# Unequal token split by a runtime branch, forget bias inside the exponential, PV by query rows, and projections between attention units

## What is computed

```python
h = rmsnorm(x, norm_g)
z = h @ w_in                     # 2048 -> 7176 columns: q k v (1024 each) f (8) gA u vB gB (1024 each)
logf = log_sigmoid(z_f + b_f)    # one forget value per token and head
s = q.k * 128**-0.5 + cum[t] - cum[s]      # cum: running sum of logf; causal, 8 heads x 128
att = softmax(s) @ v
out_a = att * silu(gA)
out_b = gelu(u) * (W_s @ layernorm(gelu(vB)) + b_s) * silu(gB)  # W_s lower triangular, 128x128, chunks of 128
y = rmsnorm(x + concat(out_a, out_b) @ w_out, final_g)
```

## Time and profile before

| | |
|---|---|
| median of 3 runs | 1996.45 us (1995.67 to 2056.99) |
| the profiled execution, span of its slowest core | 1993.9 us (cores: 1979.1 to 1993.9) |
| PE / PE weight load / DVE / ACT / POOL busy | 1786.0 / 916.8 / 790.0 / 724.4 / 209.4 us |
| bytes moved by the core's DMA queues | 187.73 MB, mean 94 GB/s |
| instructions | 31025 |

### The profile page before, as it was taken

The page is one execution under the profiler, slowest core; times in us unless marked ns, Lnnn a source line. Parts: engine busy times, 40 slices in busy tenths (PEclk is TensorE's granted clock), DMA queues, the critical chain, the costliest instruction groups (busy, mean ns, idle before and its releaser), DMA issues.

```text
span 1993.9 us, 31025 instructions; the slowest of 8 cores (1979.1 to 1993.9 us)
## 1 busy us (share of the span) xinstructions
PE 1786.0 (90%) x10577; PEld 916.8 (46%) x10721; DVE 790.0 (40%) x1349; ACT 724.4 (36%) x1303; POOL 209.4 (11%) x221
## 2 busy tenths in 40 slices
PE   2699999999999999999899958888888888879997
PEld 1255554555545555444455534444344444434443
DVE  0122222333332000144222347778777877623333
ACT  1134443222212121355222216666566655411111
POOL 4011111000021111033100000110111011100000
PEclk9799999999999999999999989999999999989999
DMA  7965664444459666100532042541453155344342
GB/s 162 151 170 159 174 167 131 96 95 104 105 79 152 101 94 101 40 1 1 55 33 21 1 80 64 97 81 28 86 97 76 26 93 75 74 139 157 139 169 90
DMA packets 220978, 187.73 MB, mean 94 GB/s; under 512 B 180688, under 2 KB 192480, under 8 KB 211408
## 3 DMA queue, kind: packets, MB, share of 16 engines
q1 hardware_dynamic: 110472, 139.56, 25.2%
q0 software_dynamic: 110352, 46.18, 20.5%
HBM read 172.12 MB, written 59.65 MB: 116 GB/s over the span
## 4 chain that ended last, share of the span: by engine, by line
PE 77%; DVE 11%; DMA 5%; issue 3%; ACT 1%; POOL 1%; DVEq 0%; SPq 0%; another core or an unknown queue 0%; ACTq 0%; POOLq 0%
PE psb L684 22%; PE psb L440 12%; PE psb L1183 11%; PE psb L430 11%; DVE arena L1093 6%; PE psb L741 6%; PE psb L1068 4%; PE psb L994 3%; PE psb L992 3%; DMA arena<-w_in 3%; PE psb L1072 1%; PE psb L415 1%; DVE arena L1044 1%; DVE arena L1039 1%; DMA arena<-w_out 1%
## 5 line engine op out<-in xcount | busy, mean ns | idle before, releaser
L684 PE MATMUL psb<-arena 128*128 128x416 bf16 (+1 forms) x2560 | 451.6, 339 | 8.7 <-ACT arena L697 5.5
L1032 ACT ACTIVATE arena<-psb 128x512 bf16<-128x512 f32 (+3 forms) x656 | 307.4, 534 | 145.7 <-DVE arena L1039 79.0
L684 PEld LDWEIGHTS psb<-arena 128*128 128x128 bf16 x2560 | 250.4, 98 | 206.3 <-issue 12.9
L440 PE MATMUL psb<-arena 128*128 128x512 bf16 (+1 forms) x1024 | 248.4, 382 | 19.0 <-DMA arena<-w_in 16.4
L1068 PE MATMUL psb<-arena 128*128 128x512 bf16 (+3 forms) x615 | 217.8, 355 | 43.0 <-ACT arena L1032 42.2
L992 PE MATMUL psb<-arena 128*128 128x512 bf16 (+3 forms) x618 | 219.7, 356 | 37.1 <-DVE arena L1039 33.5
L1183 PE MATMUL psb<-arena 128*128 128x512 bf16 (+1 forms) x1067 | 236.5, 382 | 17.8 <-DMA arena<-w_out 16.5
L994 PE MATMUL psb<-arena 128*128 128x512 bf16 (+1 forms) x639 | 227.0, 355 | 24.7 <-DMA arena<-ones_b 23.6
L430 PE MATMUL psb<-arena 128*128 128x512 bf16 (+1 forms) x1024 | 233.3, 385 | 10.2 <-DMA arena<-w_in 5.7
L1183 PEld LDWEIGHTS psb<-arena 128*128 128x128 bf16 (+1 forms) x1088 | 106.5, 98 | 148.1 <-issue 21.8
L430 PEld LDWEIGHTS psb<-arena 128*128 128x128 bf16 (+1 forms) x1056 | 102.7, 99 | 129.9 <-issue 16.0
(11 more groups left out here) (169 smaller groups left out, 1605.1 us busy)
## 6 DMA issues: line engine op xcount, KB each, us to landing
arena<-x_own SPq DMA_DIRECT2D x32, 1024.0 KB, 8.1
arena<-x_oth SPq DMA_DIRECT2D x16, 1024.0 KB, 7.9
arena<-w_in POOLq DMA_DIRECT2D x32, 512.0 KB, 7.9
y_own<-arena SPq DMA_DIRECT2D x16, 1024.0 KB, 4.8
arena<-w_in POOLq DMA_DIRECT2D x48, 256.0 KB, 27.5
arena<-KT_s SPq DMA_DIRECT2D x8, 1028.0 KB, 5.5
k_own<-arena SPq DMA_DIRECT2D x16, 512.0 KB, 4.8
v_own<-arena SPq DMA_DIRECT2D x16, 512.0 KB, 3.1
```

The costliest lines, as they stand in the source:

```text
L440: PE.op(lambda k=k, c=c: nc.tensor.matmul(PSB[4 + c][0:rows, :], hT[:, k, :], WV[:, k, c * 512:(c + 1) * 512], start=(k == 0), stop=(k == ...
L684: PE.op(lambda k=k, b=b, c0=c0, n=n: mm(PSB[b][:, 0:n], ring[s][:, k, :], H[:, k, c0:c0 + n], start=(k == 0), stop=(k == KC - 1)), reads=r ...
L1032: ACT.op(lambda: nc.scalar.activation(out=Pb[pi][0:rows, off:off + n], in_=PSB[b][0:rows, off:off + n], func=AF.Exp, scale=SCALE), reads=[ ...
```

## The change

The kernel is rewritten. Two core types ("roles") are in one program; `emit` is called for both behind a runtime branch on an input, `role`. Two cores share one stream as before: role 0 owns blocks 0 to 19 and no samples, role 1 owns blocks 20 to 31 and two sample streams (32 rows, `NS2`). Causality lets role 0 do without K and V of blocks 20 to 31; role 1 computes K and V of all 32 blocks. The host hands over x also transposed, and the weights cut and laid out by chunk.

- **Norm and K/V**: x comes transposed (`xT`), 2 blocks a load pair into three tiles; squares on ACT, sums on DVE, over partitions by f32 matmuls with ones, `rsqrt` as exp(-0.5 ln); 16 DVE multiplies make h. No transposes. K is made transposed, two heads x 256 tokens a unit; role 0 makes K of all its blocks first, then V. V is stored with a 129th column of 2.0.
- **gMLP v, u, gB, mixing**: as before, without q and gA; silu is made as (1 + tanh(x/2)) x, the factor 2 taken out elsewhere. They come before q and gA now.
- **Sweep**: no bias matmul and no mask matmul: exp has scale and a per-partition bias (`nb`, per query tile, key block and head), POOL zeroes above the diagonal. PV has P as the stationary operand, 128 query rows at a time, and V with its 129th column moving: the output has queries on partitions, its last column is twice the denominator. `fin` normalises and gates, `tr` transposes back, the result goes to HBM (`oT_s`).
- **Projections between units**: q and gA of head h+1 are cut into single matmuls (`qga`, a generator) and are emitted between the units of head h (`fill`). gA has tokens stationary and 128 weight columns moving.
- **Output**: as before, its left operand loaded from `oT_s` in groups of 4 blocks; output weights are loaded during the sweep as space comes free.

```diff
-    def e_S(i): ...  PE.op(... KTh x Qh ...); PE.op(... A_all x Bh, the bias ...); if diag: PE.op(... mneg_b ...)
-    def e_PV(i): ... PE.op(lambda: mm(PSB[ab][:, off:off + n], Vh[p][:, u["kb"], :], Pb[pi][:, off:off + n], ...
+    rv = nc.values_load(io["role"], min_val=0, max_val=1,
...
+    with nc.If(rv == 0):
+        emit(ctx, 0)
+    with nc.Else():
+        emit(ctx, 1)
...
+    if role == 0:
+        groups = [("own", list(range(4 * i, 4 * i + 4))) for i in range(NT)]
+        passes = [("K", i) for i in range(NT)] + [("V", i) for i in range(NT)]
...
+    NKS = 3                      # buffers Kf (f32) and Kb (bf16) of K units
...
+    def norm_b(n):
...
+        for c in range(2):
+            mmop(PSB[7][:, 0:w], ones[:, :], ssp[:, c, 0:w], c == 0, c == 1, [ones.r, ssp.r], 7, c == 0, c == 1)
+        ACT.op(lambda: act.activation(out=r[:, 0:w], in_=PSB[7][:, 0:w], func=AF.Ln, scale=1.0 / D, bias=RMS_EPS),
...
+        for k in range(KC):
+            DVE.op(lambda k=k: v.scalar_tensor_tensor(out=dst[:, k, :]..., in0=x[:, :, k, :], scalar=gcol[:, k:k + 1], in1=r[:, 0:w]..., 
...
+    def k_unit(gi, i0, cnt, heads):
...
+                mmop(PSB[bank][:, hi_ * w:(hi_ + 1) * w], WK[h][:, k, :], hv[:, k, :], ...
...
+            ACT.op(lambda: act.activation(out=Kf[s][:, 0:tot], in_=PSB[bank][:, 0:tot], func=AF.Copy),
...
+            POOL.op(lambda: g.tensor_copy(out=Kb[s][:, 0:tot], in_=Kf[s][:, 0:tot]), reads=[Kf[s].r], writes=[Kb[s].r])
...
+            store(SP, io["kT"]..., fv, Kf[s].r)
...
+            for i0 in (0, 2):
+                need_pair(gi, i0)
+                for h in range(0, 8, 2):
+                    if h == 4:
+                        norm_slot()          # norm_b of the next pair, x_next() (loads), norm_a of the one after
...
+                    k_unit(gi, i0, 2, [h, h + 1])
...
+    def qga(h):
...
+                mmop(PSB[b][:, 0:n], w[:, k, :], H[:, k, c0:c0 + n], ...          # q, 512 (role 1: 392) columns
+                    yield n / 2.4 + 3
...
+                    mmop(PSB[b][0:rows, i * 128:(i + 1) * 128], H[:, k, j * 128:j * 128 + rows], w[:, k, :], ...   # gA, 128 columns
+                        yield 56
...
+    LA = 2
...
+    def e_S(i):
...
+        b = i % 2
...
+            mmop(PSB[b][:, off:512], KTh[p][:, j * 128:(j + 1) * 128], Qh[p][:, T * 512 + off:(T + 1) * 512], True, True,
...
+            ACT.op(lambda: act.activation(out=P[:, off:512], in_=PSB[b][:, off:512], func=AF.Exp, scale=SCALE, bias=nb[:, T, j, h:h + 1]),
...
+            if dd >= 0:
+                POOL.op(lambda: g.affine_select(out=P[:, off:off + 128], ...
...
+    def e_PV(i):
...
+            for q in range(q0, 4):
+                b = ob + q // 2
+                mmop(PSB[b][:, (q % 2) * 256:(q % 2) * 256 + 129], P[:, q * 128:(q + 1) * 128], Vh[p][:, j, :],
...
+    def fill(finish=False):
...
+        filler["credit"] += filler["rate"]
+        while finish or filler["credit"] > 0:
...
+                filler["credit"] -= next(filler["gen"])
...
+            if i % nu_head == 0:
+                fill(finish=True)
+                if h == 7:
+                    A.free(H, *ring)
+                    f_setup()
+                else:
+                    filler.update(gen=qga(h + 1), credit=0.0, rate=fcost / (nu_head - 2))
...
+            e_S(i)
+        if i >= LA:
+            e_PV(i - LA)
+        flush(i - LA)
+        fill()
```

More of the change, by code:

```diff
@@ new lines, in v_unit @@
+        store(SP, io["V_s"].rearrange("h t j c -> t h j c")[:, :, j, :], Vb[s][:, :, :], Vb[s].r, R_Vs)
+    x_next()
+    for h in range(8):
+        load(POOL, WK[h][:, :, :], io["wk"][h], WK[h].r)
+    load(SP, bfb[:], io["bf"].partition_broadcast(128), bfb.r)
+    if smp:
+        POOL.op(lambda: g.memset(Vn[:, :, 128:129], 2.0), pwrites=[Vn.r])
+    load(POOL, wf[:, :, :], io["wf"], wf.r)
+    for c in range(len(WV)):
+        for hf in range(2):
+            load(POOL, WV[c][:, hf * 8:(hf + 1) * 8, :], io["wv"][c][:, hf * 8:(hf + 1) * 8, :], WV[c].r, part=(hf == 1))
@@ new lines, in emit, with ring_fill @@
+    assert state["pos"] == len(order)
+    A.free(*(Kb + Vb))
+    if role == 0:
+        A.free(*(Kf + Vf))
+    else:
+        A.free(*(xt[0:2] + sq + [ssp] + rb + hTb))
+    chunks = []
+    for gi in range(8):
+        chunks += [("wu", gi), ("wgb", gi)]
+    for h in range(8):
+        chunks += [("wq", h), ("wga", h)]
+    ring = [A.alloc("ring%d" % s, [KC, 128], BF16) for s in range(NRING)]
+    ring_state = {"loaded": 0, "used": 0}
+    def ring_fill():
+        while ring_state["loaded"] < min(len(chunks), ring_state["used"] + NRING):
+            i = ring_state["loaded"]
+            nm, idx = chunks[i]
+            load(POOL, ring[i % NRING][:, :, :], io[nm][idx], ring[i % NRING].r)
+            ring_state["loaded"] += 1
@@ new lines, in emit @@
+    for (rows, a, b) in parts:
+        ACT.op(lambda: act.activation(out=tzf[0:rows, a:b], in_=tzf[0:rows, a:b], func=AF.Ln, bias=1.0), reads=[R_L], writes=[R_L])
+    for (rows, a, b) in parts:
+        DVE.op(lambda: v.tensor_scalar(out=tzf[0:rows, a:b], in0=tzf[0:rows, a:b], scalar1=-1.0, scalar2=None, op0=ALU.mult),
+               reads=[R_L], writes=[R_L])
+    store(SP, io["lf"][:, o0:o0 + no, :], tz[:, o0:o0 + no, :], R_L)
+    if smp:
+        store(SP, io["lfs"], tz[0:NS2, kb, :], R_L)
+        lfc = A.alloc("lfc", [2, 16, 8], F32)
+        load(SP, lfc[:, :, :, :], io["clf"].rearrange("s p j h -> p s j h"), lfc.r)
@@ new lines, in mixing @@
+            DVE.op(lambda: v.tensor_tensor(out=t[:, 0:n], in0=t[:, 0:n], in1=Ub[p][:, c0:c0 + n], op=ALU.mult), reads=[t.r, Ub[p].r], writes=[t.r])
+            DVE.op(lambda: v.tensor_tensor(out=o[:, 0:n], in0=t[:, 0:n], in1=Gb[p][:, c0:c0 + n], op=ALU.mult), reads=[t.r, Gb[p].r], writes=[o.r])
+            store(SP, io["oT_s"][8 + gi, :, c0:c0 + n], o[:, 0:n], o.r, R_oT[8 + gi][ti])
+    for gi in range(8):
+        c_chunk("wu", gi)
+        if gi >= 1:
+            mixing(gi - 1)
+        c_chunk("wgb", gi)
@@ L1192, in build_program @@
         so = 40 + p * 4
-        ss, sd, rs = [sml[0:rows, so + i:so + i + 1] for i in range(3)]
-        ACT.op(lambda: nc.scalar.activation(out=junkF[0:rows, :], in_=yb[p][0:rows, :], func=AF.Square, accum_out=ss),
-               reads=[R_yb[p]], writes=[R_junkF, R_ssF[p]])
-        ACT.op(lambda: nc.scalar.activation(out=sd, in_=ss, func=AF.Sqrt, scale=1.0 / D, bias=RMS_EPS), reads=[R_ssF[p]], writes=[R_ssF[p]])
-        DVE.op(lambda: v.reciprocal(out=rs, in_=sd), reads=[R_ssF[p]], writes=[R_ssF[p]])
@@ L1249, in make_in_maps @@
+            ckT=c(cache_k[sm].transpose(0, 2, 3, 1)), cvn=c(cache_v[sm].reshape(2, 16, 128, 8, 128).transpose(0, 3, 2, 1, 4)),
+            clf=c(cache_lf[sm].reshape(2, 16, 128, 8).transpose(0, 2, 1, 3)))
+        for r in range(2):
+            mr = dict(m)
+            mr["role"] = np.full((1, 1), r, np.int32)
+            in_maps.append(mr)
     return in_maps
```

1958 lines of the change are left out of this document (910 added, 1048 removed).

## The result

The changed kernel takes 1659.12 us (median of 4 runs, 1657.52 to 1662.02) against 1996.82 before: ratio 0.8311, 95% interval 0.8298 to 0.8324. The forecast was 1625 us, its range 1560 to 1740. The profiled execution spans 1655.4 us.

What follows compares the result with a forecast made beforehand. TensorE bounds the kernel, 90% busy, with DVE holding the sweep. Role 0: 858 us to the sweep, 468 for it, 10 wait, 277 output, 10 tail make 1623, plus 2.5: 1625 us; range 1560 to 1740.

Steps and rivals of the forecast that it cites:

- The mechanism: Whole kernel: fewer matmul columns on TensorE and a sweep no longer held by DVE; 371 us less.
- Rival (b): Matmuls of 128 or 129 columns: slower in long streams, at most +192 us, 1817; chance 0.08.
- (a): K pass: DMA-bound at the old mean of 168 GB/s, 27.4 us a pair, +67, 1692; chance 0.14.
- (c): Sweep: projections hide nothing, units keep the old 0.90 us pace, 679 instead of 468, 1836; chance 0.07.
- (d): Sweep: TensorE waits so often that its clock is halved; heads 0 to 6 +416, 2041; chance 0.04.
- the unseen cost: Table reloads, named with a K period of 23 us for the own range's upper end, 1670 us.
- V 146 (stores 16 MB, 110 GB/s, hidden): V pass of role 0: 20 blocks at 7.29 us of TensorE, 146 us, its stores hidden.
- B to C keeps its stall of about 8 us: Before the sweep: the last LayerNorm chain still frees the space, so TensorE waits about 8 us.
- The SP loop: K pass: x loads wait for the norm, kT stores queue behind, ACT's copy waits for them; 20 us a pair.
- a DVE loop: K pass: the norm's multiplies and sums on DVE's path allow 16 to 17 us a pair at best.
- the 65 that I had set as a limit: Sweep: the forecast is wrong if a head takes over 65 us.
- Role 1 was wrong: Split of cores: role 1 needs about 1420 us of TensorE, ends near 1545; role 0 longest by some 80.

Runs made afterwards that it cites:

- The layout experiment: Changed kernel with V's scratch laid out by token, 2064 bytes a run instead of eight runs of 258: 1626.55 us.
- the late weights: Changed kernel with role 0 issuing gMLP v's weights (8.4 MB) after 12 V units instead of ahead of them: 1648.2 us.
- the late loads: Changed kernel with x loads issued after a pair's last K unit, and sums of squares as two additions: 1637.21 us, one execution.
- the combination: Changed kernel with V scratch by token, wsf moved, sums as additions, late x loads, transposes in the finished tile's bank: 1597.21 to 1600.08 us.
- the 8-row matmul of zeros: Changed kernel with a second matmul, 8 rows of zeros, into each unit's score bank, at the forget-bias matmul's place: 1889.02 us.

## Why the prediction was right, and where it was not

**The mechanism and the size were right**: the forecast was 34 us short of 1659, 2%. TensorE's sum for role 0 was 1473; PE is busy 1493.5. Part of the closeness is luck: in the table by stage the rows that ran over make 59 us together and those that ran under 27.

**Rival (b), slow narrow matmuls, is out.** The end of head 0's q and all its gA, one piece of the chain:

```profile
851.47 24.30 PE psb L291 x349
```

29 matmuls of 512 at 0.2166 are 6.3 us; the 18.0 left over 320 of 128 columns are 0.0563 each, within 2% of the short burst's 0.0556 in the earlier trace rows. The Trainium skill ("TensorE: Matmul & The Clock Gate", section Back-to-back issue gap) has about 81 ns there; the measurement decides against it for this stream.

**Rivals (a), (c), (d).** The K pass took 19.6 us a pair on the average of nine, not 27.4. In its steady part, 91 to 200 us, the DMA engines moved 170 GB/s, 3.1 MB a pair and not 4.6, at a share of 0.50: they were not the bound there, though they were nearly full in the two long pairs (0.98 and 0.87). The projections hide the units' latencies: undoing it costs 91 us. The granted clock is 1.00 in heads 0 to 6, with PE busy 94% of the time (I had said over 95), and 0.95 in head 7, with 79%: nothing like the half speed of (d).

**No table reloads in the sweep**, the unseen cost I bounded at 42 us: one load ahead of 480 exponentials and 40 tanh.

```profile
L1026 ACT ACT_TABLE_LOAD x1 | 1.3, 1283 | 0.0
```

**The step that failed: "V 146 (stores 16 MB, 110 GB/s, hidden)".** I costed the stores by bytes, and left out the 8.4 MB of gMLP v's weights that come in beside them. By runs they were 20,137 packets of under 512 bytes, at a share over 1.0 with 136 GB/s moved. The layout experiment takes the V stall away, all but 3.3 us of the second, and 37 us off core 4; the late weights moved the V stall with them, so the short runs stalled TensorE only together with the weights. The Trainium skill ("DMA: Bandwidth & Descriptors", section Specifications) names 512 bytes as the least for line rate and so speaks against this store; the traces agree (2.0 against 9.5 us for the same bytes). "B to C keeps its stall of about 8 us" found its successor one stage earlier: before gMLP v, 16.4 us, by an overlay of buffers that I had not followed. The 8 us I had kept after gMLP v for the last LayerNorm chain were not needed: u, gB and mixing ran 9 under. The row that I took them from did not name that chain either: it gives 5.5 of its 8.7 us to ACT's L697 and 3.2 to a load of w_in.

**The K pass** came near (176 us for nine pairs, 180 forecast) by luck. The SP loop that I described is there (the late loads show it), but the period was shared with a DVE loop whose sums I had 0.7 us too low each, and both were about 18. Two waits of some 20 us for a kT store, in no term of mine, made up the difference.

**The sweep**: a head took 63.3 us, under the 65 that I had set as a limit, 61.2 forecast. PE's busy time was as summed (59.5 a head, 59.4 forecast); it sat idle 3.8 us a head where I had allowed 1.8. Of that, 1.9 is its wait behind the copy of transposed tiles, which I did not name, and 0.8 its wait for the diagonal mask on POOL. A full exponential took 687 ns, not 630: I had added the 0.09 to 0.537, busy time over count, and not to the row's mean of 0.607. It cost nothing where PE sets the pace and up to 3 us (60 times 0.057) in head 7.

**Role 1 was wrong**: I had it end 80 us before role 0, and it ended 9 to 22 before. PE is busy 1488.5 us on core 1, 68 more than my sum; some 30 of these lie in 910 to 1455, where PE is busy 520 and my prices make about 490. I never laid role 1 out stage by stage, and which of its operations were costed too low is not settled. The forecast stood since role 0 still ended last; the combination ends on role 1.

## What to carry to other kernels

Cost a transfer by its runs as well as its bytes: 258-byte runs took nearly five times as long as 2064-byte ones and slowed the other transfers beside them. They stalled TensorE once a bulk load came on top, and they can be put on the side that has time. When a cut to a loop gives nothing, look which wait has grown in its place and cut both before giving it up. Follow a new buffer to what lay there before: its first write inherits the waits of all that still reads it.

## What the runs showed of the hardware that I had not expected

A matmul whose operands have 8 rows (partitions), between matmuls of 128 rows, cost about twice a matmul of 128 rows. Core 4 with the 8-row matmul of zeros, heads 0 to 6 and head 7:

```profile
876.00:1474.00 598.00, 572.86 (x5127) 324.67 (x5222) 118.28 (x307) 280.35 (x451) 51.38 (x157) 1.00 0.18 41
1474.00:1556.00 82.00, 79.40 (x349) 31.98 (x356) 11.35 (x36) 38.52 (x63) 8.72 (x26) 0.53 0.34 92
```

From the first exponential to the last tanh heads 0 to 6 took 599.3 us, 158 more than in the changed kernel: 0.38 us for each of 420 such matmuls, at a granted clock of 1.00; with 128 rows it was 515.6 us, 0.18 each. In head 7, without the projections, the granted clock was 0.53, near the lower level, although PE counts as busy for 79.40 of 82 us. With 128 rows the same head, from 1400 to 1438 us, had PE busy for 33.02 of 38 us at a clock of 1.00.

The starts in the trace tell where the time goes (the ends of matmuls are modelled). The weight load of the 8-row matmul and the next one stand apart, with the weight loader idle before each (PEld of core 4 in order of time):

```profile
1037.45 0.09 PEld L291 LDWEIGHTS psb<-arena 8*128 8x128 bf16 x1 [0.26 <-issue]
1037.76 0.90 PEld L291 LDWEIGHTS psb<-arena 128*128 128x128 bf16 x16 [0.23 <-issue]
```

From the start of the score matmul to that of the 8-row one it is 0.31 us, and 0.32 from there to the next (medians of 263); with 128 rows both are 0.216. So about 0.1 us goes ahead of the 8-row matmul, where its own streaming cannot be the cause, and about 0.1 behind it, which makes up the 0.2 between 0.38 and 0.18. That points to the changes between 8 and 128 rows; for the second part, slower streaming of the 8 rows is not excluded. The Trainium skill ("TensorEngine Tiling (Array Packing)", section Key Properties) has it that changing the tiling mode drains TensorE. A drain at each change would fit these gaps, but no record here names a mode.
